# Turning the rows of the third attention pass one step earlier

## The chip, the cores and the metric

The kernel runs on one core of a Trainium2 chip. The metric is the time of one execution on the device in microseconds (us), as the median of several. The engines go by these names: TensorE (PE in the profile; PEld is its weight load), VectorE (DVE), ScalarE (ACT), GpSimd (POOL) and SyncE (SP). Each runs its own list of instructions in order, and they wait for each other on semaphores.

## The reference

The model is two transformer blocks of two layers each, in float32, over 1024 rows of width 1024. Only one piece matters here, the first layer's mixer: dilated window attention in three groups of six heads, whose outputs are weighted against each other by their log-sum-exps, gated, and projected.

```python
DIL_GROUPS = ((128, 1), (512, 4), (2048, 16))
def mixer_dilated(u, w_in, w_out, rel_bias):
    q, k, v, gate = jnp.split(u @ w_in, 4, axis=-1)      # each 18 heads of 64
    outs, lses = [], []
    for g, (window, dil) in enumerate(DIL_GROUPS):
        hs = slice(g * HEADS_PER_GROUP_A, (g + 1) * HEADS_PER_GROUP_A)
        o, l = dilated_window_attention(q[:, :, hs], k[:, :, hs], v[:, :, hs], rel_bias[:, hs], window, dil)
        outs.append(o)
        lses.append(l)
    wts = jax.nn.softmax(jnp.stack(lses, axis=0), axis=0).astype(u.dtype)
    o = jnp.concatenate([outs[g] * wts[g][..., None] for g in range(len(DIL_GROUPS))], axis=2)
    y = o.reshape(B, S, WIDTH_A) * jax.nn.silu(gate)
    return y @ w_out
```

## The kernel before

The program is written out by hand for each engine. A float32 product is made from three products of rounded parts: every operand has a high part (`thi`, `whi`) and a low part (`tlo`, `wlo`), and "high part" and "low part" below mean these.

The first mixer is three passes, g = 0, 1, 2 (`pe_dilated`, `act_dilated`, `dve_dilated`). Each pass first makes the queries and keys of its six heads. Then it goes through 48 units, u = 6j + h: eight blocks j of 128 rows, six heads h. The loop counter i is called a step; the work of one unit is spread over steps, so that the engines overlap:

- TensorE, in step i, in this order: in even steps the scores of units i and i+1 (`da_k`,`da_q`; two PSUM banks take turns, ring `s3`); the transpose of unit i-2's exponents (`da_s`); the value product of unit i-3 (`da_p`,`da_v`); in pass 2, a turn, if `turn_at(i)` names one (line 986); then the dense multiplications of `dense_steps`, which make value tile j+2 (operands `whi`, `wlo`) and the gates of block j (`da_gh`, `da_gl`). A block has 16 dense pieces of three multiplications, or 8 in the last two blocks, where no value tile is left to make. The six steps of a block get 2, 3, 3, 2, 3, 3 of the 16 pieces, or 1, 1, 2, 1, 1, 2 of the 8.
- VectorE, in step i: adds the bias to the scores of unit i and takes the minimum (line 156), which frees the scores' bank; in odd steps a copy of turned exponents; in steps 6, 12, ... the gate of the block before: add one, reciprocal (line 159), product; in steps 8, 14, ... the product of the block's attention output with the gate (`da_y`); and in pass 2 `dve_combine`, last in the step.
- ScalarE, in step i: the exponents, copies, the gate's exponent at the end of a block, and in pass 2 `act_combine`, last in the step.

Pass 2 also weights the three groups' outputs. The rows of the first two passes lie in DRAM and come back block by block into `y01` (`da_yr` in the profile; `act_y_load` issues it on ScalarE's queue in steps 12, 18, ..., and it waits for the second turn of the block before). In step 8+6j VectorE computes the weights of block j, scales the three sets of rows by them, and signals `y_scaled`. The scaled block of 128 rows x 1152 columns is then turned in three groups of 4, 4 and 1 transposes (`TURNS`), which all use one PSUM bank (ring `a3`, bank 7). For a group, TensorE waits for `y_scaled` and for the bank (`pe_y_turn`, `pe_turn`); ScalarE copies the high part out (`act_y_hi`); VectorE subtracts it to get the low part (`dve_y_lo`, the instructions `tlo<-ps,thi`), which frees the bank. ScalarE does its part in the step of the turn, VectorE one step later, at the start of `dve_combine`. Block 7 is turned after the loop, inside the output projection (`pe_out`).

SyncE issues the loads of weights into a ring of 11 slots; GpSimd splits them into the two parts. The loads of the output projection's weights wait for slots that the last value weights of pass 2 free.

Of the kernel before, what the change touches and what calls it, by code (L numbers as in the profile page):

```python
# [273 lines left out]
class Kernel:  # L274
# [733 lines left out]

    def turn_at(self, i):

        j, n = (i - 10) // 6, (i - 10) % 6
        return (j, n // 2) if 0 <= j < 7 and n % 2 == 0 else None


# [2256 lines left out]
```

How the kernel before makes its waits and increments, by code:

```python
    def wait_ge(self, name, value):  # L123
        if self.passed.get(name, 0) < value:
            self.passed[name] = value
            if self.e is not None:
                self.e.wait_ge(self.sig.sems[name], value)
# [398 lines left out]
    def sync_program(self, q):  # L526
        self.sp_dilated(q)
        self.sp_out(q, "a")
        self.sp_latent(q)
        self.sp_heads(q)
        self.sp_out(q, "b")
        for l in range(2):
            self.sp_mix(q, l)
            self.sp_out(q, ("m", l))
            self.sp_mlp(q, l)
        for j in range(8):
            q.wait_ge(*self.S.at(f"st{j}", ("f", 1)))
# [58 lines left out]
    def load(self, sp, key, pieces):  # L596
        n = self.wn
        self.wn += 1
        self.W[key] = n
        s = n % NS
        for event in self.freeing.get(s, []):
            sp.wait_ge(*event())
        width = 0
        for c, ap in pieces:
            ww = int(np.prod(ap.shape[1:]))
            sp.dma_start(self.wst[:, s, c:c + ww], ap).then_inc(*self.S.up(f"w{s}", key, 16))
            width = max(width, c + ww)
        self.wide[key] = width
        self.freeing[s] = [lambda: self.S.at("tile", ("w", key))]
# [4 lines left out]
    def split(self, pool, key):  # L615
        s, w = self.slot(key), self.wide[key]
        pool.wait_ge(*self.S.at(f"w{s}", key))
        pool.tensor_copy(self.whi[:, s, 0:w], self.wst[:, s, 0:w]).then_inc(*self.S.up("w_hi", key))
        pool.wait_ge(*self.S.at("w_hi", key))
        pool.tensor_tensor(self.wlo[:, s, 0:w], self.wst[:, s, 0:w], self.whi[:, s, 0:w],
```

## Time and profile before

| | |
|---|---|
| median of 3 runs | 4108.52 us (4107.71 to 4110.42) |
| the profiled execution | 4107.71 us |
| its span, first to last instruction | 4105.9 us |
| mean granted TensorE clock | 0.976 of full speed |
| TensorE busy | 3868.8 us, 94% |
| VectorE, ScalarE, GpSimd busy | 2208.9, 1434.0, 1908.3 us |
| pass 2 of the dilated attention, without its projections | about 612 to 732 us of the span |

The profile is of one execution. The granted clock is that of TensorE, 1.00 for 2.4 GHz and 0.50 for 1.2 GHz. Busy time counts an engine's instructions as they overlap; idle time of an engine costs something only where others wait for it.

### The profile page before, as it was taken

What the parts mean: (1) busy time and instruction counts of PE and PEld (TensorE: products, weight loads), DVE (VectorE), ACT (ScalarE), POOL (GpSimd) and SP (SyncE); (2) the same over time, 40 slices, a digit from 0 to 9 for tenths busy, and PEclk for the clock granted to TensorE, in tenths of its full rate; (3) what the DMA queues carried; (4) which work ended last, traced back from release to release, by engine and by line L of the source; (5) the groups of instructions that cost most, each with busy time, mean ns of one, the idle gap of its engine ahead of it and who ended that gap; (6) DMA issues with size and microseconds to landing.
All of it is one profiled execution on the core that took longest, in us unless ns stands there. A gap on an engine that the chain in (4) does not pass through costs nothing.

```text
span 4105.9 us, 49866 instructions
## 1 busy us (share of the span) xinstructions
PE 3868.8 (94%) x19191; PEld 3128.8 (76%) x19191; DVE 2208.9 (54%) x3486; ACT 1434.0 (35%) x2926; POOL 1908.3 (46%) x1709
## 2 busy tenths in 40 slices
PE   8999999989999999998898999999998898999998
PEld 4677788777888887786576788888885576788887
DVE  2242427472777765324738777634415737777633
ACT  1122223133666662213534333312213634333211
POOL 1313132362333334522044788986522135787985
PEclk9999999999999999998999999999998999999999
DMA  5312221222000003110023222453210032222543
GB/s 176 116 52 81 64 61 44 93 89 65 7 9 9 9 6 113 61 35 14 1 94 97 82 80 86 151 169 128 89 31 11 1 102 89 82 85 85 168 158 130
DMA packets 247508, 310.37 MB, mean 76 GB/s; under 512 B 38804, under 2 KB 161060, under 8 KB 247272
## 3 DMA queue, kind: packets, MB, share of 16 engines
q1 hardware_dynamic: 214456, 231.87, 18.3%
q10 hardware_dynamic: 32816, 75.32, 5.3%
q8 instruction: 152, 2.49, 0.2%
q14 instruction: 84, 0.69, 0.1%
HBM read 253.48 MB, written 51.53 MB: 74 GB/s over the span
## 4 chain that ended last, share of the span: by engine, by line
PE 72%; DVE 17%; ACT 5%; issue 4%; POOL 2%; DMA 1%; ACTq 0%; SPq 0%; DVEq 0%; POOLq 0%
PE ps L130 69%; DVE cst_sm L153 3%; PE ps L133 3%; DVE ml_p L142 3%; ACT thi L136 2%; DVE da_sg L159 1%; DVE tlo L142 1%; POOL wlo L142 1%; DVE f_ta L150 1%; POOL mix_z L142 1%; ACT ml_o L136 1%; DVE f_tb L150 1%; DVE tfl L150 0%; ACT tfi L136 0%; POOL whi L139 0%
## 5 line engine op out<-in xcount | busy, mean ns | idle before, releaser
L139 POOL CAST whi<-wst 128x512 fp32r<-128x512 f32 (+3 forms) x524 | 421.7, 805 | 1284.5 <-DMA wst<-in_a_w_in 453.3
L142 POOL TENSOR_TENSOR wlo<-wst,whi 128x512 fp32r<-128x512 f32 (+2 forms) x650 | 926.7, 1433 | 42.1
L130 PE MATMUL ps<-whi,thi 128*128 128x512 f32 (+3 forms) x1816 | 694.9, 383 | 9.6 <-POOL wlo L142 3.1
L130 PE MATMUL ps<-whi,tlo 128*128 128x512 f32 (+3 forms) x1816 | 685.0, 377 | 0.0
L130 PE MATMUL ps<-wlo,thi 128*128 128x512 f32 (+3 forms) x1816 | 684.9, 377 | 0.0
L130 PEld LDWEIGHTS ps<-whi,thi 128*128 128x128 f32 x1816 | 345.5, 190 | 89.1 <-issue 22.0
L130 PEld LDWEIGHTS ps<-whi,tlo 128*128 128x128 f32 x1816 | 344.5, 190 | 56.9
L130 PEld LDWEIGHTS ps<-wlo,thi 128*128 128x128 f32 x1816 | 345.1, 190 | 55.7
L130 PE MATMUL ps<-thi,whi 128*128 128x512 f32 x856 | 339.3, 396 | 21.3 <-POOL wlo L142 17.7
L130 PE MATMUL ps<-tlo,whi 128*128 128x512 f32 x856 | 337.4, 394 | 0.0
L130 PE MATMUL ps<-thi,wlo 128*128 128x512 f32 x856 | 337.2, 394 | 0.0
L153 DVE TENSOR_REDUCE cst_sm<-ps 128x1 f32<-128x1024 f32 (+7 forms) x256 | 246.2, 983 | 35.2 <-PE ps L130 35.0
L130 PEld LDWEIGHTS ps<-thi,whi 128*128 128x128 f32 x856 | 163.5, 191 | 59.0 <-POOL wlo L142 20.6
L130 PE MATMUL ps<-mla_kh,thi 128*128 128x512 f32 x512 | 191.3, 414 | 1.9 <-ACT tfi L136 1.9
L150 DVE SCALAR_TENSOR_TENSOR f_tb<-f_ub,tfi,f_tb 128x1024 f32<-128x1024 f32 x88 | 191.6, 2177 | 1.6
L130 PEld LDWEIGHTS ps<-thi,wlo 128*128 128x128 f32 x856 | 163.3, 191 | 34.7
L130 PEld LDWEIGHTS ps<-tlo,whi 128*128 128x128 f32 x856 | 163.6, 191 | 33.8
L136 ACT ACTIVATE thi<-ps 128x512 fp32r<-128x512 f32 (+2 forms) x258 | 140.3, 566 | 118.8 <-PE ps L133 113.9
L136 ACT ACTIVATE whi<-wst 128x512 fp32r<-128x512 f32 x126 | 70.5, 620 | 279.2 <-DVE wst L142 241.4
L142 DVE TENSOR_TENSOR tfl<-c_rn,cst_rope 128x64 f32<-128x64 f32 (+1 forms) x96 | 28.2, 334 | 248.3 <-ACT c_rn L136 247.0
L142 POOL TENSOR_TENSOR tlo<-tfl,thi 128x512 fp32r<-128x512 f32 x96 | 151.8, 1587 | 6.1 <-ACT thi L136 1.1
L130 PE MATMUL ps<-c_k,c_q 64*128 64x512 f32 (+3 forms) x384 | 118.2, 610 | 29.5 <-ACT tfl L136 28.8
(379 smaller groups left out, 8240.5 us busy)
## 6 DMA issues: line engine op xcount, KB each, us to landing
wst<-in_w_down SPq DMA_DIRECT2D x140, 256.0 KB, 3.2
wst<-in_w_up SPq DMA_DIRECT2D x126, 256.0 KB, 3.0
scr_h<-f_tb SPq DMA_DIRECT2D x44, 512.0 KB, 3.9
wst<-in_w_in SPq DMA_DIRECT2D x64, 256.0 KB, 2.7
wst<-in_a_w_in SPq DMA_DIRECT2D x72, 192.0 KB, 2.4
wst<-in_ada_w SPq DMA_DIRECT2D x48, 256.0 KB, 3.3
da_am<-in_ada_w SPq DMA_DIRECT2D x48, 256.0 KB, 2.6
f_T2lw<-scr_h SPq DMA_DIRECT2D x48, 256.0 KB, 3.7
```

Source lines behind the costliest of these rows:

```text
L130: return self.none if self.e is None else self.e.matmul(*a, **k)
L133: return self.none if self.e is None else self.e.transpose(*a)
L136: return self.none if self.e is None else self.e.activation(*a, **k)
L139: return self.none if self.e is None else self.e.tensor_copy(*a)
L142: return self.none if self.e is None else self.e.tensor_tensor(*a)
L150: return self.e.scalar_tensor_tensor(out=out, in0=a, scalar=s, in1=b, op0=o1, op1=o2, **k)
L153: return self.none if self.e is None else self.e.tensor_reduce(*a, **k)
L159: return self.none if self.e is None else self.e.reciprocal(*a)
```

## The change

`turn_at(i)` says which group of which block is turned in step i. Its origin goes from 10 to 9. Group n of block j is turned in step 9+6j+2n, where it was 10+6j+2n, for blocks 0 to 6. All turns were in even steps and are in odd ones. Three callers use the function: TensorE (line 986) and ScalarE (line 1269) in step i, VectorE (line 1286) one step after. The tests `i >= 10` and those of the reload and the weights are as before.

```diff
@@ -1008,7 +1008,7 @@
     def turn_at(self, i):
 
-        j, n = (i - 10) // 6, (i - 10) % 6
+        j, n = (i - 9) // 6, (i - 9) % 6
         return (j, n // 2) if 0 <= j < 7 and n % 2 == 0 else None
```

## Rows read from the trace of the kernel before

**Rows 1.** The page's first line.

```profile
span 4105.9 us, 49866 instructions
```

**Rows 2.** Busy time by stretch: pass 2, and before and behind it.

```profile
core 0: us, PE busy (x) PEld busy (x) DVE busy (x) ACT busy (x) POOL busy (x), PEclk, DMA share, GB/s
...
531.00:612.00 81.00, 80.30 (x367) 67.83 (x368) 14.87 (x24) 17.25 (x21) 29.11 (x37) 0.98 0.27 75
612.00:732.00 120.00, 107.68 (x636) 94.64 (x635) 83.69 (x255) 43.53 (x161) 25.25 (x28) 0.93 0.14 41
732.00:800.00 68.00, 68.00 (x302) 56.28 (x301) 20.73 (x30) 3.88 (x7) 23.48 (x21) 1.00 0.31 103
```

**Rows 3.** The chain of waits, steps 18 to 24: start us, us, what.

```profile
647.41 0.27 DVE da_s L156
...
648.00 2.56 DVE da_sg L159
...
651.06 0.28 DVE da_s L156
...
651.55 0.60 DVE tlo L142
...
652.85 0.47 DVE da_y L142
...
654.75 1.02 DVE da_yr L142 x2
655.77 0.20 DVE da_s L156
...
661.35 0.27 DVE da_s L156
```

**Rows 4.** TensorE's timeline, steps 18 to 22: start us, us, then the instruction.

```profile
646.87 0.49 PE L130 MATMUL ps<-da_k,da_q 64*128 64x128 f32 x4
...
647.46 0.33 PE L130 MATMUL ps<-da_v,da_p 128*128 128x64 f32 x2
647.63 0.39 PE L133 MATMUL ps<-cst_ident,da_yr 128*128 128x128 f32 x2
...
647.99 0.42 PE L130 MATMUL ps<-whi,thi 128*128 128x384 f32 x1
...
649.24 0.33 PE L130 MATMUL ps<-da_v,da_p 128*128 128x64 f32 x2
649.38 0.42 PE L130 MATMUL ps<-whi,thi 128*128 128x384 f32 x1
...
651.15 0.74 PE L130 MATMUL ps<-da_k,da_q 64*128 64x128 f32 x4
...
652.29 0.42 PE L130 MATMUL ps<-whi,thi 128*128 128x384 f32 x1
...
654.19 0.42 PE L130 MATMUL ps<-da_gh,thi 128*128 128x384 f32 x1
...
655.42 0.49 PE L130 MATMUL ps<-da_k,da_q 64*128 64x128 f32 x2
```

**Rows 5.** The chain of waits, step 32, the scaling of the stored rows.

```profile
684.98 2.49 DVE da_yr L142 x2
```

**Rows 6.** TensorE's restarts after gaps (in brackets), and the stretches behind four gaps.

```profile
291.13 0.59 PE L130 MATMUL ps<-da_k,da_q 64*128 64x192 f32 x2 [1.92 <-DVE da_y L156]
...
303.86 1.30 PE L130 MATMUL ps<-da_v,da_p 64*128 64x64 f32 x4 [2.65 <-DVE da_p L139]
...
504.78 0.59 PE L130 MATMUL ps<-da_k,da_q 64*128 64x192 f32 x2 [1.59 <-DVE da_y L156]
...
713.49 0.48 PE L130 MATMUL ps<-da_k,da_q 64*128 64x128 f32 x2 [1.38 <-DVE cst_sm L156]
...
291.00:295.00 4.00, 3.87 (x23) 3.12 (x23) 1.99 (x10) 1.97 (x8) 0.00 (x0) 1.00 0.14 51
303.90:310.60 6.70, 6.70 (x17) 5.34 (x18) 0.56 (x1) 0.00 (x0) 0.00 (x0) 0.50 0.60 169
504.80:508.80 4.00, 4.00 (x16) 3.64 (x17) 1.36 (x6) 2.03 (x8) 0.00 (x0) 0.57 0.14 51
...
713.50:717.00 3.50, 3.50 (x20) 2.83 (x20) 3.26 (x15) 1.50 (x7) 0.00 (x0) 1.00 0.00 0
```

## The prediction

> **What bounds the kernel now.** I read the page first: the profiled execution took 4107.71 us for a span of 4105.9 us [rows 1], so 1.8 us lie around the span; the median of the runs is 4108.52, 0.8 us above that execution. I sum against 4107.7. The change touches the third pass of the dilated attention alone, so I looked next at stretches [rows 2]. Before that pass TensorE is busy 80.3 of 81 us, after it 68.0 of 68. In the 120 us of the pass it is busy 107.7, with a mean granted clock of 0.93. So the pass is the loose stretch between two that TensorE fills, and what it gains or loses goes to the end unchanged: in the 68 us behind it there is no idle time to absorb it.
>
> In the pass I followed the chain of waits through one block of six steps [rows 3]. It is a closed loop of two legs, 13.94 us long (647.41 to 661.35). I call the start of VectorE's work of a step that is a multiple of six X, and the end of the scaling of a block's rows (what `y_scaled` signals, in the step two later) Y. In these rows X is 647.41 (step 18), Y is 655.77 (step 20), and the next X is 661.35 (step 24).
> Leg B, X to Y, 8.36 us, is all VectorE: bias-and-minimum, gate, reciprocal 2.56 us, gate product, the next reduction, the low part of a turned group (0.60), the weights, the three scalings.
> Leg A, Y to the next X, 5.58 us, is all TensorE: it picks up when VectorE has freed a bank, and must get through steps 22 and 23 before it can give VectorE the scores of step 24.
>
> The timeline of TensorE in the same block [rows 4] shows what it does under leg B: dense multiplications of steps 18, 19, 20 and 21, nearly without idle time. It arrives at 655.42 at step 22, and Y is 655.77. It is late by nothing and early by almost nothing. The two engines hand over to each other, and each one's work under the other's leg is hidden.
>
> **The change part by part.** `turn_at` is asked by three engines. All 21 turned groups of blocks 0 to 6 move one step earlier; nothing is added or removed. In TensorE's step the order is scores, transpose, value product, turn, dense multiplications; so a group that was behind the dense work of step n-1 is now ahead of it. The first group of a block goes from step 10+6j to 9+6j, the second from 12+6j to 11+6j, the third from 14+6j to 13+6j. What they wait for stays: the first for Y, the second and third for the bank of the group before, which VectorE frees with the low part.
>
> *First group, start of leg A.* Before, TensorE did the dense work of step 21 (654.19 to 655.42, 1.23 us with the pause before the scores) while VectorE worked towards Y. After, the group stands ahead of it and waits for Y: TensorE is through with its value product at about 654.19 and would wait 1.6 us. All that is queued behind it on TensorE waits too, so the dense work comes behind Y, onto leg A: +1.23. The reduction that TensorE waited for at Y, 0.20 us, no longer precedes: -0.20. The group's own time is on leg A either way.
>
> *Second group, end of leg A.* It goes from behind the scores of step 24 (where leg B had begun, so it was hidden) to ahead of the dense work of step 23: + 0.36 us (647.63 to 647.99). Its bank is freed long before, so no wait.
> Leg A: +1.23 +0.36 -0.20 = +1.39 us. The dense work of that step is six multiplications in blocks 0 to 4 and three in blocks 5 and 6 (there are no value tiles left to make); three are worth 0.53 less: +0.86. Together 5 x 1.39 + 2 x 0.86 = 8.7 us.
>
> *Third group, leg B.* VectorE makes the low part of the second group one step earlier too: at the end of its step 18, behind the gate's reciprocal, not in step 19. The same 0.60 us in the same leg, but TensorE's third group now stands in step 19, ahead of nine dense multiplications, and waits for that bank. This is the step that I think costs most. The low part ends at X + 3.65 (647.41 to 651.06, where the reduction is now) + 0.60 = X + 4.25. TensorE would have got there at about X + 1.5 (649.24 plus the end of the product, less the 0.36 of the second group that is gone). It stands for 2.7 us. Then turn and start, 0.14 (651.55 + 0.60 to 652.29); nine multiplications with the pause before the scores, 1.77 (649.38 to 651.15); scores to the end of the value product of step 20, 0.92 (646.87 to 647.46 + 0.33). VectorE must have that product for the rows of the block; before, it never waited for it. From there to Y it is as now, 2.92 (652.85 to 655.77), and the low part of the third group, a quarter of the size of the 0.60 one, has moved in front of the weights: 0.2, between 0 and 0.60. X to Y = 4.25 + 0.14 + 1.77 + 0.92 + 2.92 + 0.2 = 10.2, against 8.36: +1.84. With three dense multiplications instead of nine (blocks 4 and 5) it is 1.07 less, +0.77. Block 6 has none behind its third group and the output projection starts when the last value product is in: zero. Together 4 x 1.84 + 2 x 0.77 = 8.9 us.
>
> *What costs nothing.* The high parts on ScalarE (busy 43.5 of 120 us) come one step earlier, in each case after the exponent that others want, except in step 23, where the second group's is queued before the next exponent; that one is wanted two steps later. The reload of the two stored rows stays where it is in ScalarE's queue, behind the second group. SP's and GpSimd's queues are not passed. GpSimd's splits of the output weights slow VectorE in one block, where the scaling of the stored rows takes 2.49 us and not 1.02 [rows 5]; they are released by value weights that the same dense work frees, so they move along with it and meet the same leg. If the meeting were missed, up to 4 us come back; if it is doubled, 4 are added.
>
> Sum at full clock: 8.7 + 8.9 = 17.6 us.
>
> *The clock.* TensorE gets six new gaps of 2.7 us or more and seven of about 1.1 to 1.6. Here is what gaps did in this trace [rows 6]: after 2.65 us without work the granted clock stood at 0.50, the lower level of 1.2 GHz, for 6.7 us; after 1.59 us the mean of the next four was 0.57; after 1.92 us it stayed at 1.00, and after 1.38 too. So a gap of 2.7 us most likely lowers it, and one of 1.1 hardly. The work behind the third group, 1.77 + 0.92 us, is on the path: if it all runs at half clock it costs up to 2.7 more. The lower level may start late or end early (0.57 and 0.50), so I take half of that, 1.3, in the four long blocks, and 0.7 in the two short ones, 6.6 us in all. Its bounds are 0 and 14.
>
> The Trainium skill (TensorE: Matmul & The Clock Gate, "HAM oscillation — how this bites in real kernels") tells of a loop that lost its clock in the wait of every iteration and paid half of the low time for it. By that, six low stretches of 6.7 us would cost 20 us and the time would be 4145; with my halves it is 4132. The rows here bear out that such gaps lower the clock, though not each one. Rival 3 comes near to that reading.
>
> Forecast: 4107.7 + 17.6 + 6.6 = 4132 us.
>
> **The rivals.**
> 1. *The clock holds.* For it: the gap of 1.92 us that changed nothing. Against: 2.65 and 1.59 us, which did. 4107.7 + 17.6 = 4125.
> 2. *The third group's wait is covered*: VectorE would make the low part sooner than I read it, or the value product of step 20 would still be in time. Then leg B gains only the 0.2 us. 4107.7 + 8.7 + 6 x 0.2 = 4118. Against it: `dve_combine` comes behind the gate in VectorE's step, and the reciprocal is 2.56 us.
> 3. *The clock stays low through leg A too.* The gap before Y follows within some 6 us of the one at the third group, and low stretches of 6.7 us reach from one to the other. Leg A's 7 us of TensorE work at half clock would add up to 7 us a block; in half of the seven blocks, with a quarter of the work at full clock anyway, some 18 us: 4150.
> 4. *Not slower.* Y is already there when TensorE comes to the first group, because TensorE and not VectorE is the later one. It decides when Y comes 1.6 us earlier than in these rows. Then the first group costs nothing, and at best the 0.60 us of a low part per block finds slack outside leg B, with 7 x 0.6 us gained: 4103. For it: the slack at 655.42 is only 0.35 us, so a small shift could turn the order. Against: the turn stands 1.2 us of dense work earlier, and the chain has the same form in all blocks.
> That the change does nothing can't be: all three engines place the groups by this function.
>
> **How the numbers follow.** The forecast 0.55, rival 1 0.18, rival 2 0.08, rival 3 0.13, rival 4 0.06. The range reaches from rival 2's 4118 to 4146, three quarters of the way to rival 3. A measurement of this kernel tells about 0.2%, 8.2 us, from no change: the line is at 4116.7. Slower: everything but rival 4 and a small part of rival 2, 0.91; within: 0.07; faster: 0.02.
>
> **What the profile after would show.** The pass is 20 to 28 us longer and the rest as long. The distance from one reciprocal to the next goes from 13.94 to about 17.2 at full clock, up to 18.5. TensorE has a wait for VectorE's low part ahead of the last transpose of a block, 2.7 us, six times, and one for the scaled rows of 1.1 to 1.6. VectorE's idle time before the reduction of step 20 grows, released by TensorE. The granted clock of the pass falls from 0.93 to about 0.8. If the waits at the third group are under 1 us, the largest step is wrong; if the clock is at 0.93 or more, the term for it; if the blocks are not longer, the reading of the loop.

## The result, and the profile after

The changed kernel took 4135.56 us as the median of four runs (4132.24 to 4148.02), the kernel before, beside them, 4108.86 (4107.71 to 4110.42). The ratio is 1.007, with an interval of 1.0049 to 1.0092: it is slower, by 27 us where 24 were forecast. The profiled execution took 4136.29 us, its span is 4134.5, and the instructions are as many as before.

Busy time by stretch of the kernel after, which answers to [rows 2]; the window for the pass is 28 us longer, and the same three stretches are shown:

```profile
core 0: us, PE busy (x) PEld busy (x) DVE busy (x) ACT busy (x) POOL busy (x), PEclk, DMA share, GB/s
531.00:612.00 81.00, 80.86 (x370) 68.42 (x371) 14.53 (x24) 17.78 (x23) 30.02 (x38) 0.98 0.27 75
612.00:760.00 148.00, 115.43 (x647) 100.30 (x646) 86.49 (x256) 43.75 (x159) 24.12 (x27) 0.87 0.12 38
760.00:828.00 68.00, 68.00 (x305) 56.35 (x304) 22.42 (x30) 4.36 (x5) 25.25 (x22) 1.00 0.28 94
```

TensorE is still filled before and behind the pass. In the pass its idle time went from 12.3 to 32.6 us, and the mean granted clock from 0.93 to 0.87.

The chain of waits through one block, which answers to [rows 3] (start us, us, what). X is the reduction at 653.12 (653.10 in VectorE's timeline), Y the end of the scaling, 664.68:

```profile
645.01 1.03 DVE da_yr L142 x2
...
646.17 0.63 PE ps L133 x4
646.80 1.47 PE ps L130 x10
...
650.63 0.45 PE ps L133 x4
651.08 2.04 PE ps L130 x13
653.12 0.27 DVE da_s L156
...
653.70 2.56 DVE da_sg L159
...
656.76 0.69 DVE tlo L142
657.46 0.04 issue
657.50 0.33 PE ps L133
657.83 2.86 PE ps L130 x13
...
661.46 0.04 DVE da_y L142
661.49 0.44 issue
661.93 0.28 DVE tlo L142
...
663.65 1.03 DVE da_yr L142 x2
```

The loop had two legs, one of VectorE and one of TensorE. Leg B, from 653.10 to 664.68, now has TensorE in its middle. VectorE's low part of the second group ends, TensorE turns the third group (657.50), does 2.86 us of dense work and scores, and only after the value product that follows can VectorE start on the rows (661.46). Leg A, from 646.04 on, begins with a turn (646.17) and has a second (650.63) before the scores.

TensorE's timeline of the same block (start us, us, instruction; the idle time and its releaser in brackets):

```profile
646.17 0.63 PE L133 MATMUL ps<-cst_ident,da_yr 128*128 128x128 f32 x4 [1.47 <-DVE da_yr L142]
...
657.50 0.33 PE L133 MATMUL ps<-cst_ident,da_y 128*128 128x128 f32 x1 [2.62 <-DVE tlo L142]
657.58 0.42 PE L130 MATMUL ps<-whi,thi 128*128 128x384 f32 x1
...
658.54 0.46 PE L130 MATMUL ps<-whi,tlo 128*128 128x384 f32 x1
658.80 0.52 PE L130 MATMUL ps<-whi,thi 128*128 128x384 f32 x1
```

The stretches right behind four of the gaps at the third group (columns as above; the clock stands before the DMA share):

```profile
638.80:642.40 3.60, 3.60 (x15) 3.23 (x16) 0.78 (x7) 0.88 (x4) 0.00 (x0) 0.62 0.00 0
657.50:661.50 4.00, 4.00 (x18) 3.34 (x19) 1.11 (x9) 1.32 (x7) 0.00 (x0) 0.64 0.00 0
676.10:680.00 3.90, 3.86 (x17) 3.43 (x18) 0.99 (x7) 0.88 (x4) 0.00 (x0) 0.62 0.02 4
...
733.90:743.00 9.10, 8.27 (x32) 6.69 (x33) 4.53 (x22) 2.62 (x10) 0.00 (x0) 0.50 0.01 3
```

All seven waits at the third group are of 2.6 to 3.1 us, and each is followed by a stretch at the lower level. It starts up to some 1.3 us after TensorE has gone on (at 696.2 behind the wait that ends at 694.93), or shortly before: in the block above, multiplications of 384 columns take 0.33 to 0.34 us behind the first one, and from 658.54 on 0.46 and 0.52. The waits of 1.2 to 1.5 us at the first group are followed by none in the four long blocks.

### The profile page after: what moved, and what is told of

The parts are those of the page before. It is cut to its first block, busy times and chain, and to the rows that moved or that the text cites. A ratio compares the mean times of both kernels' runs of the same rounds, so it can differ in the third digit from the quotient of the medians.

```text
span 4134.5 us, 49866 instructions
## 1 busy us (share of the span) xinstructions
PE 3880.9 (94%) x19191; PEld 3135.0 (76%) x19191; DVE 2196.6 (53%) x3486; ACT 1434.1 (35%) x2926; POOL 1900.4 (46%) x1709
## 3 DMA queue, kind: packets, MB, share of 16 engines
q8 instruction: 152, 2.49, 0.2%
## 4 chain that ended last, share of the span: by engine, by line
PE 71%; DVE 17%; ACT 5%; issue 4%; POOL 1%; DMA 1%; ACTq 0%; SPq 0%; DVEq 0%; POOLq 0%
PE ps L130 68%; PE ps L133 4%; DVE cst_sm L153 3%; DVE ml_p L142 3%; ACT thi L136 2%; DVE da_sg L159 1%; DVE tlo L142 1%; DVE f_ta L150 1%; DVE f_tb L150 1%; POOL mix_z L142 1%; ACT ml_o L136 1%; ACT tfi L136 0%; DVE tfl L150 0%; DVE cst_sm L150 0%; ACT p_p L136 0%
## 5 line engine op out<-in xcount | busy, mean ns | idle before, releaser
L130 PE MATMUL ps<-thi,whi 128*128 128x512 f32 x856 | 339.6, 397 | 16.3 <-POOL wlo L142 12.7
L136 ACT ACTIVATE tfi<-ps,cst_sm 128x1024 f32<-128x1024 f32 (+1 forms) x160 | 130.2, 814 | 45.2 <-PE ps L130 24.6
```

Source lines behind the costliest of these rows:

```text
L130: return self.none if self.e is None else self.e.matmul(*a, **k)
L136: return self.none if self.e is None else self.e.activation(*a, **k)
```

## Leg by leg, all kernels

This table is worked out from VectorE's timelines: X is the start of the reduction ahead of the gate, Y the end of the second scaling of the stored rows. "Pass" is the distance from the start of the first of the eight reciprocals to that of the last. Leg A stands for the turns of blocks 1 and 2 (in "first group alone" of block 3 too), leg B for the first three in which the third group is turned, in their order. Each row is from one execution.

| kernel | leg A, us | leg B, us | pass, us | over before |
|---|---|---|---|---|
| before | 5.56, 5.56 | 8.38, 8.38, 8.38 | 620.51 to 722.36: 101.85 | |
| after | 7.07, 7.07 | 11.64, 11.57, 11.72 | 620.00 to 747.16: 127.16 | 25.3 |
| first group alone | 7.25, 8.78, 8.78 | 8.38, 8.37, 8.38 | 625.59 to 742.34: 116.75 | 14.9 |
| second group alone | 7.00, 7.00 | 8.57, 8.57, 8.57 | 626.13 to 738.88: 112.75 | 10.9 |
| third group alone | 5.59, 5.58 | 12.29, 12.14, 10.81 | 625.03 to 743.16: 118.13 | 16.3 |
| all, third in another bank | 7.04, 7.03 | 8.77, 8.77, 8.76 | 620.79 to 737.17: 116.38 | 14.5 |
| all, wait filled | 7.09, 7.09 | 10.41, 10.43, 10.42 | 626.11 to 748.45: 122.34 | 20.5 |
| all, turned behind dense work | 6.05, 6.06 | 8.83, 8.82, 8.83 | 626.78 to 736.23: 109.45 | 7.6 |
| first alone, third in another bank | 6.62, 6.64 | 8.37, 8.38, 8.37 | 622.68 to 732.18: 109.50 | 7.7 |

The runs of one edited kernel lie 8 to 17 us apart, so the legs carry the argument and the medians only have to agree.

## The experiments

**1. The first group alone.** The changed kernel with the old steps for the other two; only the list of first steps differs between this and the next two:

```diff
-        j, n = (i - 9) // 6, (i - 9) % 6
-        return (j, n // 2) if 0 <= j < 7 and n % 2 == 0 else None
+        for n, s in enumerate((9, 12, 14)):
+            j, r = divmod(i - s, 6)
+            if r == 0 and 0 <= j < 7:
+                return j, n
+        return None
```

> Only the first group of a block is turned a step earlier; the second and third stay in the steps of the kernel before. Theory (dense work pushed behind the scaled rows): leg A grows by 1.23 - 0.20 = 1.0 us in the blocks with six dense multiplications there and 0.5 in the two with three, leg B by nothing; 5 x 1.0 + 2 x 0.5 = 6 us, 4115. Rival (the loss is all at the third group's bank): nothing, 4109. Rival (the clock falls at every gap ahead of the scaled rows): leg A runs at half clock, 3 us or more a block, over 4125.

4125.47 us (4121.96 to 4134.60), ratio 1.0045 (1.0032 to 1.0058). Leg B is as before, as expected. Leg A is 7.25 us in block 1 and 8.78 in blocks 2 and 3, where I had 6.6; in block 0, ahead of which no third group stands, it is 6.61. The chain of waits, here of block 2, shows what I had missed:

```profile
662.56 1.02 DVE da_yr L142 x2
663.58 0.20 DVE da_s L156
663.78 0.01 DVE cst_sm L156
663.79 0.20 DVE da_p L139
664.00 0.21 DVE tlo L142
664.20 0.04 issue
664.25 1.05 PE ps L133 x4
665.30 2.62 PE ps L130 x10
```

TensorE isn't released by the scaled rows but by a low part. The third group of the block before, still in its old step, has the bank, and its low part is made only in the next step, 0.6 us behind the scaling. 5.57 + 1.0 + 0.65 is 7.2, what block 1 has. In blocks 2 and 3 the clock fell as well, though the waits are about as long (2.05 and 2.03 us, 2.02 in the block where it held): the four transposes behind the wait take 1.05 us, where they take 0.63 in the changed kernel's chain, and the mean clock from 664.3 to 667.8 is 0.51. So the first group's move has a second cost, a bank wait that exists only while the third group stays late. The first rival is out. The second, 3 us or more a block for the clock, is what blocks 2 and 3 have (3.2 over before, 1.5 of it beyond block 1), though the clock didn't fall in every block.

**2. The second group alone.** `(10, 11, 14)`.

> Only the second group is turned a step earlier, in the step behind the first. Theory: its 0.36 us come onto leg A, and since the first group's low part is now made in the same step of VectorE (behind a copy that needs a transpose of that step of TensorE), TensorE stands about 0.9 us for the bank ahead of the dense work: leg A +1.3 in seven blocks, leg B +0, 9 us, 4118. Rival (only the first group's dense work and the third's bank count): 7 x 0.36 = 2.5 us, 4111.

4126.99 us (4117.94 to 4134.70), ratio 1.0042 (1.0028 to 1.0057). Leg A 7.00 us, +1.44, where the theory had 1.3; leg B + 0.2; TensorE waits seven times for a low part ahead of the turn, 0.81 us each, 5.7 us in all, one of them here:

```profile
653.38 0.44 PE L133 MATMUL ps<-cst_ident,da_yr 128*128 128x128 f32 x2 [0.81 <-DVE tlo L142]
```

The rival's +0.36 is out. The pass is 10.9 us longer, not 9.

**3. The third group alone.** `(10, 12, 13)`.

> Only the third group is turned a step earlier, behind the second one's step as in the changed kernel, but the low part of the second group stays one step later in VectorE. Theory (bank wait ahead of the dense work): the low part ends at X + 4.76, 0.5 later than I gave the changed kernel; leg B + 2.3 us in four blocks and + 1.3 in two at full clock, 11.8 us, and 1.3 or 0.7 a block of lower clock; 4120 at full clock, 4127 with it; leg A unchanged. Rival (the third group's wait is covered): 1 us, 4110.

4124.18 us (4121.91 to 4130.36), ratio 1.0039 (1.0027 to 1.0051). Leg A is as before to 0.03 us. Leg B is 10.81 us in the block where the clock held and 12.1 to 12.3 in the two where it fell, against 10.7 and 12.0 from the expectation. TensorE's wait was the same in all three, 2.63 or 2.64 us, and in the fourth long block (2.63 us), where the clock fell again. These stretches reach from the wait to behind the value product in the three blocks (the clock is the third figure from the end):

```profile
642.00:652.00 10.00, 9.13 (x48) 7.88 (x49) 5.42 (x24) 3.14 (x14) 0.00 (x0) 0.83 0.00 0
660.00:670.00 10.00, 9.25 (x49) 8.22 (x50) 5.29 (x24) 3.29 (x14) 0.00 (x0) 0.83 0.00 0
677.00:686.00 9.00, 7.53 (x47) 6.56 (x48) 6.03 (x27) 3.11 (x13) 0.00 (x0) 1.00 0.02 6
```

The rival, that the third group's wait is covered, is out.

**4. All groups early, the third in another bank.** It takes its turn among the two banks of the exponents' transposes, so that it has nothing to do with the second group's low part.

```diff
-                self.pe_y_turn(q, *self.turn_at(i), "a3")
+                self.pe_y_turn(q, *self.turn_at(i), "t3" if self.turn_at(i)[1] == 2 else "a3")
```

> The changed kernel, all three groups a step earlier, but the third group is written to one of the two banks that the exponents' transposes use in turn, so that it doesn't wait for the low part of the second. Theory: the gap of 2.6 us ahead of the third group and the clock that falls behind it vanish; leg B goes back to about 8.6 to 8.8 us from 11.6, leg A stays at 7.0; 4109 + 9.6 + 6 x 0.4 = 4121, some 13 us less than the changed kernel. Rival (leg B is longer for VectorE's own new order): leg B stays over 11 us, 4135.

4128.57 us (4124.63 to 4141.81), ratio 1.0051 (1.0036 to 1.0066). Leg B is 8.77 us and leg A 7.03, both as expected. With the wait for the bank, 2.9 us of leg B's 3.3 are gone. The rival, that VectorE's own new order lengthens leg B, is left with 0.4. The pass is 10.8 us shorter than in the changed kernel. The median is only 7 us less than the changed kernel's and almost 8 above the 4121 expected; with runs 17 us apart it neither confirms nor refutes the size.

**5. The wait filled with work.** 14 multiplications of 384 columns of which nothing is used.

```diff
             if g == 2 and self.turn_at(i):
+                if self.turn_at(i)[1] == 2:
+                    for _ in range(14):
+                        q.matmul(ps[:, 0, 128:512], self.thi[:, 0, 0:128], self.thi[:, 0, 0:384], start=True, stop=True)
                 self.pe_y_turn(q, *self.turn_at(i), "a3")
```

> The changed kernel with 14 more multiplications of 384 columns (2.4 us) ahead of each third group, into an unused part of a scores' bank; their result isn't used. They fill TensorE's gap of 2.6 us and delay nothing. Theory (part of leg B's 3.3 us is clock lost after the gap): the granted clock stays at 1.00 behind the third group and leg B is 10.2 to 10.4 us in the long blocks, not 11.6; 4 x 1.3 + 2 x 0.7 = 6.6 us less than the changed kernel, 4129, and the leg still 1.9 longer than before. Rival (the gap itself is all the cost): leg B stays at 11.6, 4135.

4133.48 us (4125.50 to 4135.61), ratio 1.0053 (1.0040 to 1.0065). TensorE's timeline around the filled wait, and the stretches behind three of them:

```profile
641.96 0.33 PE L130 MATMUL ps<-da_v,da_p 128*128 128x64 f32 x2
642.10 2.68 PE L130 MATMUL ps<-thi 128*128 128x384 f32 x14
644.91 0.33 PE L133 MATMUL ps<-cst_ident,da_y 128*128 128x128 f32 x1
```

```profile
644.90:648.90 4.00, 3.99 (x25) 3.62 (x26) 2.21 (x13) 1.54 (x7) 0.00 (x0) 1.00 0.00 0
662.40:666.40 4.00, 3.99 (x25) 3.62 (x26) 2.20 (x13) 1.54 (x7) 0.00 (x0) 1.00 0.00 0
679.90:683.90 4.00, 3.98 (x25) 3.61 (x26) 2.20 (x13) 1.54 (x7) 0.00 (x0) 1.00 0.01 4
```

The clock stays at 1.00, in 4 us TensorE does 25 matmuls and not 18, and leg B is 10.42 us, where it was 11.6. The third group starts when it did (X + 4.41, after X + 4.40). So of leg B's 3.3 us, 2.0 are the order with its wait, and 1.2 the clock. Over all six blocks with a leg B, the changed kernel's legs sum to 6.6 us more than these. The whole pass is only 4.8 us shorter, because the legs A of this kernel sum to 1.8 us more: 9.28 and 6.47 us in blocks 4 and 5, against 8.73 and 5.18. In block 5 the clock fell here, behind a wait of 2.01 us at the first group (0.52 from 725.6 to 729.1). The median, 2 us less, doesn't resolve that by itself.

**6. The turns behind the dense work of the same step.**

```diff
-            if g == 2 and self.turn_at(i):
-                self.pe_y_turn(q, *self.turn_at(i), "a3")
             if i < 48:
                 for what, t, k in self.dense_steps(g, i):
...
                         self.pe_gates(q, g, t, k)
+            if g == 2 and self.turn_at(i):
+                self.pe_y_turn(q, *self.turn_at(i), "a3")
```

> The changed kernel, the same steps, but in a step TensorE turns behind the dense multiplications and not ahead of them. Theory (the cost is the dense work held up behind a waiting turn): the first group waits where TensorE waited anyway, leg A loses the 1.23 us and keeps the 0.36 of the second group, about 5.9; leg B has only the small low part and what is left of the bank wait, 8.6 to 8.9; 7 x 0.7 = 5 us, 4114. Rival (the cost is the earlier step itself, in all three engines): as the changed kernel, 4135.

4119.06 us (4109.36 to 4126.30), ratio 1.0019 (1.0009 to 1.0030). Leg A 6.05 us and leg B 8.83, against about 5.9 and 8.6 to 8.9 expected. ScalarE and VectorE have exactly the changed kernel's order here; what differs is what stands behind TensorE's wait. That is worth 17.7 of the 25.3 us of the pass, clock included. Of the 7.6 that are left, the long blocks 0 to 3 have 1.9 on leg A, 0.46 to 0.50 each, mostly the second group's 0.36, and the first three legs B 1.3. Block 5 has 2.9 on leg A alone (7.91 us, 5.02 before), at a mean clock of 0.51. The surplus of leg B I put down to low parts that moved in VectorE's order, and to what is left of the wait at the third group (0.96 to 1.00 us); no run takes the two apart.

**7. The first group alone, without the bank wait.** The list of experiment 1 and the bank of experiment 4.

> Only the first group a step earlier, as in the run where leg A grew to 7.25 us at full clock and 8.78 at half, but the third group goes to one of the exponents' banks, so that the first group of the next block doesn't wait for the third's low part. Theory: the first group starts with the scaled rows, leg A is 6.6 us at full clock, as first expected of that run, and no more than 7.3 where the clock falls; leg B 8.4; 6 to 10 us over the kernel before, 4116 to 4120. Rival (that leg A was long for half clock alone, whatever the bank): leg A still 8 or more in most blocks.

4119.81 us (4112.18 to 4123.08), ratio 1.0022 (1.0012 to 1.0031). Leg A is 6.62 to 6.64 us in blocks 0 to 3 and leg B 8.37. The turn now starts 0.06 us behind the scaled rows, and they release it:

```profile
645.12 0.66 PE L133 MATMUL ps<-cst_ident,da_yr 128*128 128x128 f32 x4 [1.53 <-DVE da_yr L142]
```

The 1.05 to 1.08 us that are left are what the held-up dense work was forecast to cost (1.03), and experiment 1's surplus was the third group's bank and the clock that fell with it.

## Why the prediction was right, point by point

**The loop of two legs.** Right. Every kernel shows it, and each edit moved the leg that it should. That a lengthening of the pass goes to the end in full is right too: 24.8 us stand at the last reciprocal of the pass (722.36 to 747.16), still 24.8 some 76 us later (the reciprocal at 798.83, now 823.61), and 28.6 at the end. The 3.8 us beyond arise later, in work that the change doesn't touch, where the mean granted clock is 0.97 and not 0.98; what lowered it there stays open. The medians of the kernel before differ by 2 us from one set of runs to another. So the near hit of the time has a share of luck, and the pass is the better measure: 25.3 us, 24.2 forecast.

**First group, +1.03 us.** Right: 1.05 to 1.08 in experiment 7. In the changed kernel the third group is early as well, so the bank wait of experiment 1 doesn't arise. The prediction never looked at that bank, and got its number right only because the three move together.

**Second group, +0.36, and no wait.** Right in the changed kernel: leg A is longer by 1.50 in the long blocks, 1.39 forecast. With experiment 7's 1.05 to 1.08 for the first group, 0.42 to 0.45 are left for the second; 0.08 of that is that the turn starts 0.14 us behind the scaled rows here and 0.06 there. The wait that experiment 2 shows is one of the second group moved by itself.

**Leg A in sum.** 8.7 us forecast, 9.6 measured, but the blocks differ from their terms and make up for each other. Blocks 0 to 3 have 1.5 each (1.39 forecast), block 4 has 0.8 (1.39) and block 5 has 0.2 (0.86); in the kernel before, the clock was at 0.50 until 706.6, well into block 5's leg (704.46 to 709.48), and in the changed kernel it is 1.00 there. The last block has 2.6 and not 0.9: 7.15 us from Y to the last reciprocal, where it had been 4.51. TensorE ran at a clock of 0.50 from 733.9 to 743.0, past its wait at the first group at 740.16. That is the form of rival 3, for one block out of seven. But the low level doesn't have to come from the third group's wait: in experiment 5 that wait is filled, the clock is 1.00 behind it and falls only in leg A, behind the 2.00 us at the first group, and the leg has 7.03 us all the same:

```profile
741.56 0.63 PE L133 MATMUL ps<-cst_ident,da_yr 128*128 128x128 f32 x4 [2.00 <-DVE da_yr L142]
```

```profile
736.50:740.50 4.00, 3.06 (x20) 2.52 (x20) 3.16 (x17) 1.54 (x7) 0.00 (x0) 1.00 0.00 0
742.70:745.80 3.10, 3.10 (x16) 2.78 (x16) 1.40 (x6) 1.27 (x6) 0.00 (x0) 0.51 0.00 0
```

The forecast had no clock term for leg A; it allowed for one only as rival 3.

**Third group, + 1.84 at full clock.** Right: 2.04 in experiment 5. It is the largest step, as forecast, with a wait of 2.62 us where 2.7 were forecast. The sum of leg B at full clock is 9.2 us (8.9 forecast): in experiment 5 three blocks give 2.0 each, the block beside GpSimd's splits 1.8, the two short ones 0.3 and 1.0. The zero for block 6 holds in sum: its third group waits 3.08 us, but behind the last reciprocal, where TensorE had stood 3.17 us for VectorE before, and the shift of 24.8 us is the same on both sides of it.

**The clock, 6.6 us within 0 to 14.** Right at 6.6, the difference between the legs B of the changed kernel and of experiment 5; by the whole pass it is 4.8, for the legs A of experiment 5. That half of the bound would be lost was a choice and not worked out, so the exact hit is luck. What the chain shows is near to it, though: the low level began at 658.5, 1.0 us behind the turn, and the value product ended at 661.4, so about half of the 2.7 us of work was slow. The mean clock of the pass is 0.87, where about 0.8 was forecast, and from one reciprocal to the next are 18.6 to 18.8 us in the long blocks, 18.5 at most forecast. The bound of rival 1, that it holds, is out: it fell behind each of the seven waits. But in experiment 3 it held once in four behind a wait of 2.63 us, so 6.6 is what this execution had, and not a constant. The Trainium skill's loop that lost its clock in the wait of every iteration (TensorE: Matmul & The Clock Gate, "HAM oscillation — how this bites in real kernels") is what the trace of the changed kernel shows, behind waits of 2.6 to 3.1 us. But a wait cost 1.2 us, so only some 2.4 us behind it were slow and on the path, and the 20 us that I worked out by that page were too many.

**What was to cost nothing.** Neither ScalarE nor the reload stands in the chain of the block shown. TensorE has one new wait for ScalarE's copy, 0.84 us at 747.45, behind the last reciprocal, where it adds nothing to the shift. The slow scaling beside GpSimd's splits met the same leg again, 2.50 us after 2.49.

**Rivals 2 and 4.** Both out. The third group's wait was not covered. TensorE waited for the scaled rows in every block, 0.8 to 1.5 us outside the one beside GpSimd's splits, so it was always the earlier of the two.

## What to carry to other kernels

An instruction moved earlier in an engine's own order gains nothing if what it waits for doesn't come earlier too; then everything behind it on that engine waits with it, and its price is the work that used to hide under the wait. Before moving one, list for each wait what the engine did in that time, and who has the buffer now: of three moves that share a buffer, each costs something else alone than together with the others (here 14.9, 10.9 and 16.3 us of the pass alone, 25.3 together). A wait of 2.6 us can cost TensorE a second time, in the clock behind it: 1.2 us here.

## What the runs showed of the hardware

The granted clock fell behind gaps of 3 us and less: behind all seven of 2.6 to 3.1 us in the changed kernel, and not behind those of 1.2 to 1.5 us in its four long blocks. The length of the gap alone doesn't decide it. In experiment 3 it fell behind waits of 2.64, 2.63 and 2.63 us and held behind another of 2.63; in experiment 1 it fell behind 2.05 and 2.03 us and held behind 2.02. Filling the gap with work whose result isn't used kept it at 1.00 and shortened leg B by 1.2 us. That can be worth trying where a wait can't be taken away, though in the time of whole runs it was not clear of the scatter.
